# The expert grid of a PEER layer: a rounded part and a remainder, multiplied in single-pass matmuls

## The reference

```
s = einsum('nhcq,ckq->nhck', q, sub_keys)          # 8 heads, 2 halves, 128 keys each
sv, si = top_k(s, 16)
cand = sv[:, :, 0, :, None] + sv[:, :, 1, None, :]   # 256 pairs per head
top_s, top_j = top_k(cand, 16);  g = softmax(top_s)
act = gelu(einsum('ced,cd->ce', u_tab[eidx], x))
y   = einsum('ce,ced->cd', g * act, v_tab[eidx])     # 128 chosen experts per token
```

## Time and profile before

| | |
|---|---|
| median of three runs | 6790.28 us |
| profiled execution, its own time | 6796.73 us |
| its span, first to last instruction | 6794.9 us |
| TensorE busy, share of the span | 84% |
| VectorE, ScalarE, GpSimd busy | 44%, 33%, 29% |
| granted TensorE clock, mean | 0.924 of full |

### The profile page before, as it was taken

One profiled execution on the slowest core, in us unless ns is written; L12 is line 12 of the kernel. 1 busy time (PEld: TensorE's weight loads), 2 busy tenths in 40 slices (PEclk: granted clock), 3 DMA queues, 4 the chain that ended last, 5 costly groups with the idle time before them and its releaser, 6 DMA issues. The chain is left out here.

```text
span 6794.9 us, 129634 instructions
## 1 busy us (share of the span) xinstructions
PE 5731.2 (84%) x53620; PEld 5467.7 (80%) x53620; DVE 3002.7 (44%) x5298; ACT 2237.4 (33%) x2694; POOL 1991.4 (29%) x986
## 2 busy tenths in 40 slices
PE   5873875899999979999857738668999999799998
PEld 2852865899999979999837528657999999799998
DVE  4236553943232044444442365539332320444444
ACT  4222222155555522222142322221555555222221
POOL 0000310055555533333200003101555554333332
PEclk8966987999999989999979669879999999899999
DMA  4100001134444464544241000011344444644542
GB/s 184 46 13 32 5 29 60 62 115 149 145 144 147 142 224 148 161 160 149 87 171 48 8 32 5 28 60 67 117 145 147 148 146 154 208 155 154 161 151 96
DMA packets 276357, 747.84 MB, mean 110 GB/s; under 512 B 20097, under 2 KB 105473, under 8 KB 271105
## 3 DMA queue, kind: packets, MB, share of 16 engines
q1 hardware_dynamic: 275968, 742.10, 33.2%
HBM read 557.74 MB, written 184.29 MB: 109 GB/s over the span
## 5 line engine op out<-in xcount | busy, mean ns | idle before, releaser
L1677 POOL TENSOR_TENSOR tk_u_lo<-tk_u_raw,tk_u_hi 128x1024 fp32r<-128x1024 f32 x256 | 686.9, 2684 | 1559.0 <-ACT tk_u_hi L1607 1559.0
L309 PE MATMUL ex_ps_y<-ex_wa_hi,ex_v_hi 128*128 128x320 f32 x4096 | 941.4, 311 | 175.3 <-DVE ex_wa_lo L1902 175.3
L1887 POOL TENSOR_TENSOR ex_v_lo<-ex_v_raw,ex_v_hi 128x1024 fp32r<-128x1024 f32 x256 | 636.7, 2488 | 1307.8 <-ACT ex_v_hi L1863 1307.8
L309 PE MATMUL ex_ps_a<-h_hi,tk_u_hi 128*128 128x320 f32 x4096 | 963.7, 317 | 56.7 <-POOL tk_u_lo L1677 48.7
L309 PE MATMUL ex_ps_a<-h_lo,tk_u_hi 128*128 128x320 f32 x4096 | 934.8, 309 | 0.0
L309 PE MATMUL ex_ps_a<-h_hi,tk_u_lo 128*128 128x320 f32 x4096 | 934.8, 309 | 0.0
L309 PE MATMUL ex_ps_y<-ex_wa_lo,ex_v_hi 128*128 128x320 f32 x4096 | 934.7, 309 | 0.0
L309 PE MATMUL ex_ps_y<-ex_wa_hi,ex_v_lo 128*128 128x320 f32 x4096 | 934.4, 309 | 0.0
L1908 DVE TENSOR_TENSOR ex_y<-ex_y,ex_ps_y 128x640 f32<-128x640 f32 x512 | 421.0, 822 | 1014.6 <-PE ex_ps_y L309 1014.6
L309 PEld LDWEIGHTS ex_ps_y<-ex_wa_hi,ex_v_hi 128*128 128x128 f32 x4096 | 684.0, 188 | 191.8 <-DVE ex_y L1908 123.1
L309 PEld LDWEIGHTS ex_ps_a<-h_hi,tk_u_hi 128*128 128x128 f32 x4096 | 676.6, 189 | 58.7 <-POOL tk_u_lo L1677 49.6
(11 more groups left out here) (295 smaller groups left out, 8340.9 us busy)
## 6 DMA issues: line engine op xcount, KB each, us to landing
tk_u_raw<-in_expert_u SPq DMA_DIRECT2D x256, 512.0 KB, 4.2
ex_v_raw<-in_expert_v SPq DMA_DIRECT2D x256, 512.0 KB, 3.6
act_spill<-tk_act_e SPq DMA_DIRECT2D x256, 320.0 KB, 2.3
grid_scratch<-tk_grid SPq DMA_DIRECT2D x160, 512.0 KB, 5.2
ex_a<-act_spill SPq DMA_DIRECT2D x64, 1280.0 KB, 5.9
ex_g<-grid_scratch SPq DMA_DIRECT2D x64, 1280.0 KB, 9.8
mod_w<-in_w_mod SPq DMA_DIRECT2D x24, 2048.0 KB, 8.5
in_raw<-in_w_blocks SPq DMA_DIRECT2D x42, 512.0 KB, 3.6
```

Of the source, the lines that this page charges most:

```text
L309: ins = nc.tensor.matmul(out[:, q, 0:HALF], a, b[:, q * HALF:(q + 1) * HALF], start=(first and n == 0), stop=(last and n == 2))
L1677: nc.gpsimd.tensor_tensor(u_lo[:, at % 2], u_raw[:, at % 4], u_hi[:, at % 2].bitcast(F32), ALU.subtract).then_inc(e["u_split"], 1)
L1887: nc.gpsimd.tensor_tensor(v_lo[:, G * h + k], v_raw[:, k], v_hi[:, G * h + k].bitcast(F32), ALU.subtract).then_inc(e["v_split"], 1)
```

## The change

The weight g is kept in two parts: `g_hk[:, 0]`, rounded to fp32r, and `g_hk[:, 1]`, the remainder after the rounding. `on_i` gets both products, `on_j` and `on_i` become fp32r, and each token is two fp32r matmuls that accumulate in PSUM, with the same stationary operand, where it was one f32 matmul. GpSimd's `spread` issues two multiplications and signals after the second. VectorE's `keep` has one instruction more, a subtraction. To make room, `u_raw` and `ghk` move into the space of `s.x`, and `cand`, `on_j` and `on_i` get space of their own; the wait for `x_away` moves from VectorE to SP, ahead of the row loads. `hot` has one buffer where it had two.

```diff
-        hot = sb("hot", [P, 2, H, K, K], BF16)
+        hot = sb("hot", [P, H, K, K], BF16)
-        ghk = sb("ghk", [P, 3, H * K])
-        num_hk, g_hk = sb("num_hk", [P, 2, P], BF16), sb("g_hk", [P, TILES * P])
+        num_hk, g_hk = sb("num_hk", [P, 2, P], BF16), sb("g_hk", [P, 2, TILES * P], F32R)
-        u_raw = sb("u_raw", [P, 4, KB, P])
-        cand = room[:, 0:H * K * K].rearrange("p (h a) -> p h a", h=H)
-        on_j = room[:, 2048:3072].rearrange("p (u t n) -> p u t n", u=S, t=B)
-        on_i = room[:, 3072:4096].rearrange("p (u t n) -> p u t n", u=S, t=B)
+        ghk = room[:, 4 * D:4 * D + 3 * H * K].rearrange("p (c n) -> p c n", c=3)
+        u_raw = room[:, 0:4 * D].rearrange("p (r k n) -> p r k n", r=4, k=KB)
+        cand, on_j, on_i = sb("cand", [P, H, K * K]), sb("on_j", [P, S, B, P], F32R), sb("on_i", [P, S, 2, B, P], F32R)
...
                 sp.dma_start(iota[:], s.d["iota"]).then_inc(e["iota_in"], 16)
+                sp.wait_ge(s.x_away, 16)
                 for r in range(4):
                     load(r)
...
                     for t in range(B):
-                        last = nc.tensor.matmul(ps_g[:, u, t, :], on_j[:, u, t, :], on_i[:, u, t, :],
-                                                start=True, stop=True)
+                        for q in range(2):
+                            last = nc.tensor.matmul(ps_g[:, u, t, :], on_j[:, u, t, :], on_i[:, u, q, t, :],
+                                                    start=(q == 0), stop=(q == 1))
...
-                    nc.gpsimd.tensor_tensor(on_i[:, n % S], tokens_of(n // B % 2, 0, n % B), bcast(g_hk[:, at], 2, P),
-                                            ALU.mult).then_inc(e["oni"], 1)
+                    for q in range(2):
+                        last = nc.gpsimd.tensor_tensor(on_i[:, n % S, q], tokens_of(n // B % 2, 0, n % B),
+                                                       bcast(g_hk[:, q, at].bitcast(F32), 2, P), ALU.mult)
+                    last.then_inc(e["oni"], 1)
...
-                        link(v.tensor_copy(g_hk[:, at], ps_t[:, 2]))
+                        link(v.tensor_copy(g_hk[:, 0, at], ps_t[:, 2]))
+                        link(v.tensor_tensor(g_hk[:, 1, at], ps_t[:, 2], g_hk[:, 0, at].bitcast(F32), ALU.subtract))
...
-                dve.wait_ge(s.x_away, 16)
```

More of the change, by code:

```diff
@@ L1709, in _ @@
                 v = nc.vector
-                LINKS = 28
+                LINKS = 29
                 def sequence(m, link):
@@ L1725, in candidates @@
                         pair = row(best)
-                        settle(v.tensor_tensor(cand.rearrange("p h (a b) -> p h a b", a=K),
+                        settle(v.tensor_tensor(cand[:].rearrange("p h (a b) -> p h a b", a=K),
                                              bcast(pair[:, :, 0, :], 3, K), bcast(pair[:, :, 1, :], 2, K), ALU.add))
@@ L1751, in numbers @@
                     def numbers(c):
-                        link(v.tensor_tensor(hot[:, c], bcast(slot[:, c], 3, K),
+                        link(v.tensor_tensor(hot[:], bcast(slot[:, c], 3, K),
                                              bcast(bcast(iota_b[:, 0:K, 0], 1, K), 1, H), ALU.is_equal))
-                        link(v.tensor_tensor(hot[:, c], hot[:, c], bcast(row(best_f)[:, :, c, :], 2, K), ALU.mult))
-                        link(v.tensor_reduce(ghk[:, c, :].rearrange("p (h k) -> p h k", k=K), hot[:, c], AX.X, ALU.add))
+                        link(v.tensor_tensor(hot[:], hot[:], bcast(row(best_f)[:, :, c, :], 2, K), ALU.mult))
+                        link(v.tensor_reduce(ghk[:, c, :].rearrange("p (h k) -> p h k", k=K), hot[:], AX.X, ALU.add))
                     def normalise():
```

## The result

The changed kernel takes 6807.72 us (median of 20 runs) where the kernel before takes 6792.14 (20 runs): a ratio of 1.0022, 95% interval 1.0015 to 1.0029, or 15.6 us more. The forecast was 6 us more. The profiled execution took 6813.66 us; 6802.7 was forecast for it.

What follows compares the result with a forecast made beforehand. TensorE bounds the grid's stretch, busy 997.6 of 1001.5 us. Matmul pace unchanged, GpSimd hidden, starts 6 us: 6796.73 + 6 = 6802.7 us profiled, 6796.3 for the median; range 6780 to 6860.

Steps and rivals of the forecast that it cites:

- Pace of the matmuls: TensorE's groups: loads set 0.107 to 0.115 us a record against 0.111 now, so no change, 10 us either way.
- slow narrow matmul: Rival, TensorE's groups: a 128-column fp32r call costs what an f32 call does, 284 us more, 7080 us; chance 0.12.
- quick fp32r loads: Rival, TensorE's groups: loads quicker than the rows say, pace falls to 0.060 us, 131 us less, 6665; chance 0.08.
- GpSimd hidden in the stage: Inside the stage, 320 more multiplications at 1.44 us, 461 us, fit GpSimd's idle time and cost nothing.
- the late `low`: GpSimd, `numbers` chunk: `low` behind a doubled spread ends at 1907.7, its row starts at 1909.6, margin 1.9 us.
- the rival's bad case: GpSimd late in `numbers` chunks: spreads 3.46 each, `low` 5.75, so 3.6 us late, 16 times, 58 us; chance 0.12.
- The start: Each layer's start: subtraction 0.3 and second multiplication 2.7 delay group 0 by 3.0 us, 6 us in all (3.4 to 7.6).
- `low(8)`: GpSimd, layer start: behind four more multiplications, ends near 1396.3, before row 8 at 1398.1; at worst 7 us late a layer.
- "no change on TensorE": Main case: TensorE's record pace stays, only 6 us at the starts is added; chance 0.68.

Runs made afterwards that it cites:

- e3: Changed kernel with each token's second matmul narrowed, to a 64-column load (tokens 0, 1) or a 64-column stream (tokens 2, 3): 6780.15 us in one execution, ratio 0.9973.
- e5: Changed kernel with on_i, on_j and both parts of g in bf16, g kept to 16 bits: 0.9849 of the kernel before.
- e1: Changed kernel with on_i, on_j and g in f32 and one f32 matmul a token, GpSimd still multiplying twice: 1.0011 of the kernel before.
- e8: The bf16 version (e5) with TensorE loading the second key's one-hot straight from the tokens' tile, ScalarE widening nothing: 0.9940 of the kernel before.
- e6: Changed kernel with TensorE's loop over the first four tiles written out, so without a return: 0.9992 of the kernel before.

## Why the prediction was right, and where it was not

- *Pace of the matmuls: right.* No change was forecast from the load (0.107 to 0.115 us), 0.112 was measured, and e3 and e5 show the cause: cut the load and the matmuls follow each other quicker, cut the stream and they don't. The rivals of a slow narrow matmul and of quick fp32r loads are both out.
- *GpSimd hidden in the stage: right.* In the `numbers` chunk of tile 2 the late `low` ends at 1912.98, and its row starts at 1912.04 + 0.89 + 1.75 = 1914.7: a margin of 1.7 us, where 1.9 was worked out. The price behind it was partly lucky: a single `spread` took 5.27 us in that chunk, against at most 3.46 in the rows, and the two together 7.65 against 6.9 in the rival's bad case. It stayed hidden because the `low` behind them took 2.40 and not 5.75. e5 uses the margin up.
- *The start: right in its term, short in its consequence.* 3.0 us a layer forecast, 2.56 measured. What that wait does to the clock, 3 us a layer more, wasn't in the sum. `low(8)` came in time, as forecast; the text counts four multiplications more ahead of it, but three spreads stand there, so it is three, and all six took 11.71 us in place of 8.00 for three.
- *The term that was missing* is in "no change on TensorE", as far as that stood for the whole stage. I weighed whether a record gets shorter, and not that a record of the same length does half the streaming. The clock was 1.00 in the windows that I read the earlier trace rows, and I took it as given. The trace after shows 9 us of half clock at the returns of the loop and 6 at the starts, 15 us beside the 18 by which the whole stage grew, and e1, with f32 groups again, has none at the returns and less at the starts. The forecast said within 0.2% of no change, with the chance of more on the slower side; it came out on the edge, at 0.22%. That the measured 15.6 us more lies in the range is luck as far as its upper part goes: that room was kept for a pace of 0.115 us and a late `low(8)`, and neither happened.

## What to carry to other kernels

A matmul with as many columns to load as to stream is paced by the load; look at the weight load's duration for the type before counting passes, and let a cheaper number of passes go with a type that loads quickly. After a change that makes TensorE's work thinner at the same pace, look at the granted clock behind every idle gap near it, loop returns included, and in more than one execution: the same wait had half clock behind it in one version and not in another. Work on an engine that is idle on average is still paid in full at the first item of a pipeline.

## What the runs showed of the hardware

- A weight load of 128 columns: 192 ns in fp32r and f32, 98 ns in bf16 (e5); pace of the group's 128-column records 0.112 us and 0.057. With 16 elements between a bf16 load's columns, 0.073 (e8).
- The return of TensorE's loop over the tiles comes with a gap of 1.5 to 2.35 us; written out, the same instructions run without it (e6).
- At the returns, half clock behind a gap goes with the gap's length and with how fully TensorE streamed ahead of it (table above). Behind start waits of 2.3 to 2.8 us it came in 3 of 10 cases, for no reason that the runs show.
- Two multiplications of 512 elements on GpSimd take 2.8 us in quiet and 7.65 beside VectorE's work on `numbers`:

```profile
1902.98 7.65 POOL L1685 TENSOR_TENSOR tk_on_i<-tk_one_hot,tk_g_hk 128x512 fp32r<-128x512 bf16 x2
1910.58 2.40 POOL L1677 TENSOR_TENSOR tk_u_lo<-x,tk_u_hi 128x1024 fp32r<-128x1024 f32 x1
```
